# Three groups of seven block products in the feed-forward steps of a two-block transformer kernel on Trainium2

## The reference, cut to what matters

```
# D_MODEL = 2048, D_FF = 5632, SEQ = 256
h2 = rms_norm(x, g_norm2) * (1 + sc2) + sh2
x = x + gt2 * ((silu(h2 @ w_gate) * (h2 @ w_up)) @ w_down)            # first block
...
y = rms(h, norm_ffn_g_2)
h = h + (silu(y @ w_gate_2) * (y @ w_up_2)) @ w_down_2                # second block
```

## Time and profile before

| | |
|---|---|
| median of 3 runs | 2284.97 us (2284.89 to 2286.12) |
| profiled execution | span 2284.0 us, about 1 us around it up to the median |
| steps | 20, in two stretches from 536 to 1184 us and from 1524 to 2172 us |
| TensorE busy | 2234.5 us, 98% of the span |
| VectorE busy | 1894.3 us, 83% |
| ScalarE busy | 1164.2 us, 51% |
| DMA | 518.23 MB, mean 227 GB/s |
| granted TensorE clock | 0.9 or more in each of 40 slices |

### The profile page before, as it was taken

How to read it: one execution, slowest core, us unless ns; L and a number is a source line. 1 busy time by engine, 2 the same in 40 slices (tenths; PEclk the granted TensorE clock), 3 DMA queues, 4 the chain that set the end, 5 groups by cost and what they waited for, 6 DMA issues and landing times.

```text
span 2284.0 us, 30541 instructions
## 1 busy us (share of the span) xinstructions
PE 2234.5 (98%) x10404; PEld 1790.4 (78%) x10404; DVE 1894.3 (83%) x2265; ACT 1164.2 (51%) x1465; POOL 87.9 (4%) x124
## 2 busy tenths in 40 slices
PE   6999989999999999999999999999999999999998
PEld 3577657788888888888888887888888888888886
DVE  4376878989888888999995998589889999999866
ACT  3233367465445545555545444555555555555554
POOL 1100030000000000000010000000000000000020
PEclk9999999999999999999999999999999999999999
DMA  9999995856666656666656555666666566656564
GB/s 391 414 361 374 399 354 204 322 205 208 194 194 202 195 191 202 201 195 206 203 177 216 176 190 165 191 222 200 195 196 199 197 201 207 197 186 205 189 202 148
DMA packets 131565, 518.23 MB, mean 227 GB/s; under 512 B 14496, under 2 KB 20256, under 8 KB 118304
## 3 DMA queue, kind: packets, MB, share of 16 engines
q1 hardware_dynamic: 121552, 449.11, 58.8%
q0 software_dynamic: 9216, 67.11, 7.2%
q10 hardware_dynamic: 720, 0.99, 0.1%
HBM read 512.96 MB, written 4.19 MB: 226 GB/s over the span
## 4 chain that ended last, share of the span: by engine, by line
PE 77%; DVE 4%; issue 1%; ACT 1%; DMA 0%; DVEq 0%; SPq 0%; ACTq 0%
PE ps L2456 55%; PE ps L2638 20%; DVE w_lo L1930 1%; PE ps L2444 1%; PE ps L2602 1%; DVE gate L2199 1%; PE ps L2923 0%; DMA raw<-in_w_out 0%; ACT w_hi L888 0%; DVE fm_lo L1905 0%; DVE stage L1919 0%; PE ps L2332 0%; DVE ungated L1810 0%; DVE short L1382 0%; PE ps L2354 0%
## 5 line engine op out<-in xcount | busy, mean ns | idle before, releaser
L888 ACT ACTIVATE w_hi<-raw 128x1024 fp32r<-128x1024 f32 (+1 forms) x498 | 514.5, 1051 | 450.0 <-PE ps L2638 255.2
L1930 DVE TENSOR_TENSOR w_lo<-raw,w_hi 128x1024 fp32r<-128x1024 f32 (+1 forms) x248 | 299.5, 1218 | 152.4 <-ACT w_hi L888 147.5
L888 ACT ACTIVATE w_hi_more<-raw 128x1024 fp32r<-128x1024 f32 x264 | 278.9, 1056 | 209.0 <-DMA raw<-in_w_down 114.7
L2638 PE MATMUL ps<-w_lo,fm_hi 128*128 128x512 f32 (+1 forms) x896 | 347.2, 388 | 0.0
L2638 PE MATMUL ps<-w_hi,fm_hi 128*128 128x512 f32 (+1 forms) x840 | 332.1, 395 | 4.1 <-DVE w_lo L1930 2.7
L2456 PE MATMUL ps<-w_lo,fm_hi 128*128 128x512 f32 x800 | 311.3, 389 | 0.0
L2638 PE MATMUL ps<-w_hi,fm_lo 128*128 128x512 f32 (+1 forms) x776 | 300.3, 387 | 0.0
L1613 DVE TENSOR_TENSOR w_lo<-raw,w_hi_more 128x1024 fp32r<-128x1024 f32 x240 | 287.6, 1219 | 7.1
L1613 DVE TENSOR_TENSOR w_lo<-raw,w_hi 128x1024 fp32r<-128x1024 f32 x240 | 284.3, 1218 | 4.0
L2456 PE MATMUL ps<-w_lo,hid_hi 128*128 128x512 f32 x640 | 249.0, 389 | 0.0
L804 ACT ACTIVATE sum_w_hi<-sum_raw 128x1024 fp32r<-128x1024 f32 x120 | 126.9, 1058 | 174.5 <-DVE sum_raw L1640 121.9
(11 more groups left out here) (376 smaller groups left out, 3793.4 us busy)
## 6 DMA issues: line engine op xcount, KB each, us to landing
raw<-in_w_gate SPq DMA_DIRECT2D x176, 512.0 KB, 4.3
raw<-in_w_up SPq DMA_DIRECT2D x176, 512.0 KB, 3.5
raw<-in_w_down SPq DMA_DIRECT2D x176, 512.0 KB, 3.6
ada_raw<-in_w_ada POOLq DMA_DIRECT2D x64, 1024.0 KB, 10.6
raw<-in_w_in SPq DMA_DIRECT2D x120, 512.0 KB, 3.8
raw<-in_w_out SPq DMA_DIRECT2D x64, 512.0 KB, 3.6
ada_raw<-in_w_ada SPq DMA_DIRECT2D x16, 1024.0 KB, 8.4
ada_raw<-in_w_gate SPq DMA_DIRECT2D x16, 1024.0 KB, 5.8
```

The costliest lines, as they stand in the source:

```text
L888: act.activation(hi_tile(like)[:, :, 0:width], raw[:, slot, :, 0:width], ACT.Copy).then_inc(hi_ready, 1)
L1930: dve.tensor_tensor(w_lo[:, slot, :, 0:width], raw[:, slot, :, 0:width], hi_tile(p)[:, :, 0:width], ALU.subtract).then_inc(lo_dve, 1)
L2638: last = pe.matmul(banks[t][:, 0:width], a, b, start=kt == 0 and k == 0, stop=kt == kts - 1 and k == 2)
```

## The change

There are three groups, not two, so a step has 21 forms of 6 matmuls and four c pieces (270 matmuls, not 276). DVE makes four more sums and three more low parts of sums a step, ACT three more high parts. The third group's left-hand operands are made before the steps.

The work on the sums moves between engines. Before the down pieces of two banks ACT writes the running total into the banks (`sums_in`, SBUF to PSUM), PE accumulates onto it, and ACT copies the banks back (`sums_out`). DVE's `add_step` is gone. ACT applies Silu itself, DVE's `silu` is gone, and `hidden_next` is one multiplication.

The orders change too. In `early`, c1 no longer stands behind b22. In `middle`, one c piece stands in each of the first two groups, between w and z. The third group has none inside, and its w comes ahead of b21. Before the first step DVE now does `hidden_first` ahead of `early`, where it had stood inside it.

```
-GROUPS = 2
-STEP_ORDER = (("b11", 0), ("c", 0), ("v", 0), ("b22", 0), ("c", 1), ("u", 0), ("c", 2), ("b21", 0), ("w", 0), ("z", 0), ("c", 3),
-              ("b11", 1), ("v", 1), ("b22", 1), ("c", 4), ("u", 1), ("b21", 1), ("c", 5), ("w", 1), ("c", 6), ("z", 1), ("c", 7))
+GROUPS = 3
+STEP_ORDER = (("b11", 0), ("c", 0), ("v", 0), ("b22", 0), ("u", 0), ("b21", 0), ("w", 0), ("c", 1), ("z", 0),
+              ("b11", 1), ("v", 1), ("b22", 1), ("u", 1), ("b21", 1), ("w", 1), ("c", 2), ("z", 1),
+              ("b11", 2), ("v", 2), ("b22", 2), ("u", 2), ("w", 2), ("b21", 2), ("z", 2), ("c", 3))
...
+            def sums_in(i, d):
+                if d == 0:
+                    act.wait_ge(sum_copied, i * 2 + 2 * before + 2)
+                elif d == 1:
+                    act.wait_ge(drained, i + before + 1)
+                act.wait_ge(down_out, i * 4 + summed_to + (d - 3 if d < 2 else d - 1))
+                act.activation(down_banks(d), total[:, :, d * NW:(d + 1) * NW], ACT.Copy).then_inc(down_in, 1)
+            def sums_out(i, d):
+                act.wait_ge(pieces_used, i * 24 + a + 18 + 2 * d)
+                act.activation(total[:, :, d * NW:(d + 1) * NW], down_banks(d), ACT.Copy).then_inc(down_out, 1)
...
             def down_his(i):
+                down_hi(i, 0)
                 copy_first(i)
+                down_hi(i, 1)
                 copy_second(i)
+                sums_in(i, 0)
+                down_hi(i, 2, 3)
+                sums_in(i, 1)
+                down_hi(i, 4)
+                step_silu(i)
+                down_hi(i, 5)
+                sums_out(i, 0)
+                sums_in(i, 2)
+                down_hi(i, 6, 7)
+                sums_out(i, 1)
+                sums_in(i, 3)
...
-                    last = act.activation(silu_t[:, :, :], src, ACT.Tanh, scale=0.5)
+                    last = act.activation(hidden[:, :, :], src, ACT.Silu)
...
-                    last = dve.scalar_tensor_tensor(hidden[:, :, :], silu_t[:, :, :], 0.5, up, ALU.mult, ALU.mult)
+                    last = dve.tensor_tensor(hidden[:, :, :], hidden[:, :, :], up, ALU.mult)
...
-            def silu(i):
-                dve.wait_ge(tanh_done, i + done + 2)
-                dve.scalar_tensor_tensor(silu_t[:, :, :], silu_t[:, :, :], 1.0, sums[:, 0:2, :], ALU.add, ALU.mult).then_inc(silu_step, 1)
...
-            def add_step(i, d):
...
                 down_lows(i, (0,))
                 drain_forms(i)
                 up_sums(i)
-                down_lows(i, (1,))
-                down_lows(i, (2,))
+                down_lows(i, (1, 2))
                 gate_sums(i)
-                down_lows(i, (3,))
-                silu(i)
+                down_lows(i, (3, 4))
                 hidden_next(i)
+                down_lows(i, (5, 6, 7))
...
             mix_operands(1)
-            rests(f + UP + 2, f + UP + 4)
-            silu_first()
+            rests(f + UP + 2, f + UP + 3)
+            mix_operands(2)
+            rests(f + UP + 3, f + UP + 4)
...
-            first_lows(0)
+            hidden_first()
+            early(0)
```

More of the change, by code:

```diff
@@ L174, in hi_free, with last_in_place @@
     return p + 1 - (FFN_HI if f is not None and p - f >= FFN_HI else SPLIT)
-SUMMED = (("u", 0), ("v", 0), ("w", 0), ("z", 0), ("u", 1), ("v", 1), ("w", 1), ("z", 1))
+SUMMED = [(kind, k) for k in range(GROUPS) for kind in ("u", "v", "w", "z")]
 USED = [item for item in STEP_ORDER if item[0] in ("u", "w", "z")]
+def last_in_place(kind, k):
+    n, place = USED.index((kind, k)), sum_place(kind, k)
+    return next(m for m in range(n - 1, n - 1 - len(USED), -1) if sum_place(*USED[m]) == place)
 def low_by_dve(p):
@@ L426, in build @@
         unit_read, down_read = sem("unit_read"), sem("down_read")
+        down_in, down_out = sem("down_in"), sem("down_out")
         aux_filled, aux_drained = sem("aux_filled"), sem("aux_drained")
@@ L780, in act_ffn, with gate_silu, step_silu, down_banks @@
             a, before = f + 2 * UP, FFN_STEPS - 1 if done else 0
-            def gate_tanh(j, src):
+            total, summed_to = x if done else ungated, LEAD + 4 * before
+            def gate_silu(src):
                 if done:
                     for t in range(TT):
-                        last = act.activation(silu_t[:, t, :], src[:, t, :], ACT.Tanh, scale=x_half[:, t:t + 1])
+                        last = act.activation(hidden[:, t, :], src[:, t, :], ACT.Silu, scale=x_rstd[:, t:t + 1])
                 else:
-                    last = act.activation(silu_t[:, :, :], src, ACT.Tanh, scale=0.5)
-                last.then_inc(tanh_done, 1)
-            def step_tanh(i):
+                    last = act.activation(hidden[:, :, :], src, ACT.Silu)
+                last.then_inc(silu_done, 1)
+            def step_silu(i):
                 act.wait_ge(gate_read, i + done + 2)
-                gate_tanh(i + 1, sums[:, 0:2, :])
+                gate_silu(sums[:, 0:2, :])
+            def down_banks(d):
+                return ps[:, 4 + 2 * (d % 2):6 + 2 * (d % 2), :]
+            def sums_in(i, d):
[8 more added lines that the diff above has]
+                act.activation(total[:, :, d * NW:(d + 1) * NW], down_banks(d), ACT.Copy).then_inc(down_out, 1)
             def hidden_hi(n, dst=hid_hi, bank=0):
@@ L1628, in place_free @@
             def place_free(i, kind, k):
-                former = (kind, k - 1) if k and kind != "u" else (kind, k if kind == "u" else GROUPS - 1)
-                step_of = 1 if former[1] < k else 0
-                dve.wait_ge(form_used, (i + before + step_of) * 3 * GROUPS + USED.index(former) + 1)
+                dve.wait_ge(form_used, (i + before + 1) * 3 * GROUPS + last_in_place(kind, k) + 1)
             def sum_u(i, k):
@@ L1712, in middle @@
                 piece_low(i, "b21", 1)
-                piece_low(i, "c", 5)
                 sum_low(i, "w", 1)
-                piece_low(i, "c", 6)
+                piece_low(i, "c", 2)
                 sum_low(i, "z", 1)
-                piece_low(i, "c", 7)
+                sum_u(i, 2)
+                piece_low(i, "b11", 2)
+                sum_v(i, 2)
+                sum_w(i, 2)
+                piece_low(i, "v", 2)
+                piece_low(i, "b22", 2)
+                sum_low(i, "u", 2)
+                sum_z(i, 2)
+                sum_low(i, "w", 2)
+                piece_low(i, "b21", 2)
+                sum_low(i, "z", 2)
+                piece_low(i, "c", 3)
                 down_lows(i, (0,))
@@ L2451, in low_wait, with three_passes @@
                 pe.wait_ge(lo_dve if by_dve else lo_ready, i * LOWS_A_STEP[by_dve] + count)
-            def three_passes(bank, h, l, wh, wl, start, stop):
+            def three_passes(bank, h, l, wh, wl, start, stop, onto=False):
                 for k, (left, right) in enumerate(((h, wh), (l, wh), (h, wl))):
-                    last = pe.matmul(bank, left, right, start=start and k == 0, stop=stop and k == 2)
+                    last = pe.matmul(bank, left, right, start=start and k == 0, stop=stop and k == 2, skip_group_check=onto)
                 return last
@@ L2540, in down @@
                 for d in ds:
[L2541 to L2545 removed]
+                    pe.wait_ge(down_in, i * 4 + 4 * before + d + 1)
                     b = 4 + 2 * (d % 2)
```

162 lines of the change are left out of this document (63 added, 99 removed).

## The result

The changed kernel took 2382.94 us (median of 4 runs, 2381.54 to 2384.38), the kernel before 2285.36 beside it (median of 4, 2284.89 to 2286.12). The ratio is 1.0425, with a 95% interval of 1.0412 to 1.0438: slower by 4.3%. The forecast was 2371, with a range of 2345 to 2389. The profiled execution has a span of 2379.8 us, 95.8 more than before; it is the fastest of its four, and the medians lie 97.6 apart.

A forecast was written before the change was run, and what follows sets the result against it. It took DVE's written order and the turn to bound each step, not PE: 20 x 3.7 = 74 us, plus 12 at the block starts, is 86; 2285 + 86 = 2371 us, range 2345 to 2389.

The forecast's parts named there:

- The step: Each of 20 feed-forward steps: DVE's written order and the turn give 67.2 us, 3.7 more than now.
- the five places: PE waits for DVE at first b21 1.05, second v 1.3, second b21 0.6, third v 1.3, third w 0.65 us.
- DVE can't work ahead: In the down pieces DVE gets ahead only until the ring of six fills, then waits some 4 us for first v.
- the landing chain: Rival: the first v's landing, not the turn, holds DVE; 66.2 us a step, 2351 us; chance 0.09.
- the sum: Whole kernel: 20 x 3.7 = 74 for the steps and 12 for the block starts, 86 us more, 2371 us.
- a rival: The shorter chain, through the landing instead of the turn: 66.2 us a step, 2351 us; chance 0.09.
- 1.36 holds: DVE starts hid_lo 1.36 us after PE's first v, set by the turn, even with a landing of 4.8 us.
- PE as the bound: Rival: PE remains the bound in the steps, so fewer matmuls make the kernel faster, 2270 us; chance 0.12.
- ACT's queue: Rival: a PSUM copy or its wait holds a high part by 1 us; step 68.2, 2391 us; chance 0.06.
- The starts: Before each block's first step: 6.5 us more in the first block, 5.5 in the second, together 12.

The follow-up runs named there:

- the pair of extra instructions: Changed kernel plus one unused 1024-element DVE reduction a step: in the third group 2402.66 us, or between d5's and d6's low parts 2380.69 us.
- the halved low parts: Changed kernel with the low part of each sum made over 512 of 1024 elements, same number of matmuls: 2311.86 us, ratio 1.012.
- the shorter ring: Changed kernel with each transfer of the steps sent one piece later, as if the ring had five places: 2418.68 us, ratio 1.0582.
- the run with the earlier turn: Changed kernel with PE's turn of the hidden slice behind b11, not behind c0: 2367.79 us, ratio 1.0354 to the kernel before.
- the clean two groups: Changed kernel without its third group, in the orders of before, with the start and tail edits: 2286.47 us, ratio 1.0004 to the kernel before.
- the start woven: Changed kernel with `hidden_first` moved behind the low parts of b11 and c0 in each block's first step: 2372.53 us, ratio 1.0374.

## Why the prediction was right, and where it was off

**The step: right, in mechanism and size.** 67.2 was forecast and 67.24 measured; 74 us for the 20 steps against 74.5. Hid_lo starts 1.34 us behind the first v (forecast 1.36). D1 starts 43.18 behind the first v before it (863.76, and 887.82 less a step of 67.24), forecast 43.2. PE's waits by start times are 0.92, 1.15, 0.50, 1.16 and 0.52 at the five places, against 1.05, 1.3, 0.6, 1.3 and 0.65, and next to nothing at d1 (0.15). That is 4.25; the matmul behind each of these six restarts comes 0.1 later than usual, which makes 4.9 against the 5.05 of the forecast. That it is DVE's work at its place in the order that decides was shown by the pair of extra instructions (1.1 against 0) and by the halved low parts.

**DVE can't work ahead: right, with one term missing.** It waits 5.17 us for a landing, where some 4 was said, and the shorter ring made each step 2.1 us longer. The row from sum_u to hid_lo was put at 9.5 and took 10.0 in the run with the earlier turn. DVE's own instructions were sized well, 9.36; the missing term is the 0.45 for ACT's high part of the u sum. So the landing chain gives 66.7 a step, not 66.2, and in the changed kernel the turn holds DVE by 0.5 only. It didn't touch the sum, but two chains lie closer than I had them, and a rival was priced 10 us too low. The prediction also says that 1.36 holds with a landing of 4.8 too. It doesn't: 4.8 + 0.35 + 9.5 - 13.1 is 1.55.

**PE as the bound: failed, and why.** The Trainium skill (Perfetto Trace Analysis, Identifying the Most-Contended Engine) would have the engine with the highest occupancy optimized first. PE had 98%, its work fell by 1.36 us a step, and the kernel became slower. The prediction leaves out that the same section judges TensorE's headroom not by its matmuls' busy share but by its work against the peak and by the busy share of its weight loads. The share of the weight loads was 78% before, below DVE's 83%, and read so the section points at DVE. But the clean two groups took 118 us off DVE and were no faster. Neither share tells what this change does; both leave out the order in which the engines wait for each other. The sentence on consistent bubbles fits in part: PE loses the same 5 us in each step, and more when the ring is cut to five. That too few buffers make them is not shown, since they went down by 3.45 when DVE's low parts were halved, with the same ring.

**ACT's queue: hidden inside the steps, partly by luck, and wrong behind them.** Two groups with all of ACT's copies have steps as before. With three groups DVE waits 0.44 us a step for ACT's high part of the u sum, a place that the prediction does not name. It costs nothing only because the turn comes 0.47 later still. That is luck of 0.5 us, not a margin that was worked out. The copies of the running total into PSUM take 1.029 on average in the changed kernel, where 1.03 was taken. But I had looked at ACT's queue only inside a step. At the end of the last step a copy of the totals stands ahead of the high parts of the last slice, and the sum had nothing for that. 4.6 us were missing for the two tails; reordering gave 5.4 back.

**The starts: the place right, the size too small.** The forecast was 6.5 and 5.5, measured were 8.4 and 6.9. The waits are near the forecast: 0.82, 1.49 and 4.12 in the first block, 6.4 together, and 1.43 and 3.89 in the second. The missing term is the clock: behind 4 us of idle PE, b11 and c0 took 1.75 us longer. Its terms don't add up to their 6.5 either: 2.9 and 3.8, less 0.3, with 0.5 more, are 6.9. The 0.5 for a later hid_lo was not seen, the first step being 67.25 long like the others. The Trainium skill (TensorE: Matmul & The Clock Gate, What's actually happening) has half rate as the default state from which activity releases; the windows agree, with 0.50 granted behind the idle stretch. The forecast has no term for it. At the wait of 2.6 us behind the first block's last step the runs go both ways: 0.50 behind it in four profiled executions, 1.00 in four.

**The sum.** 74.5 + 15.3 + 4.6 + 1.4 is 95.8 against 86: half a us for the steps, 3 for the starts, 5 for the tails, and 1.4 that I can't tell from scatter. All of these have the same sign, so the measured time lies 12 us above the forecast of 2371, in the upper part of the range.

**What stays open.** A larger ring was not tried, so what the step would be without the landing chain is not measured. Nor was a part of DVE's low parts moved to GpSimd. Nor was another order of the same three groups: the prediction's own reading is that c pieces are where DVE catches up, and the third group has none inside. So it is not shown whether three groups must be slower, or only these three in this order. What sets their steps of 63.05 to 63.57 (PE's work with the turn is 63.46 before) was not taken apart.

## What to carry to other kernels

Where two engines hand work to each other in a written order, follow one period of it: start at an event that both share, count the instructions that stand in the queue up to each hand-over, and compare with when the other engine wants it. The sum of busy time tells only what the period can't go below; here one instruction more was free where the engine already waited for a buffer, and cost its full length in the stretch where the other engine waits for it. Then look at the two ends of the loop by themselves: what stands in an in-order queue ahead of the next part's first work, and what the granted clock is behind a wait there.

## What the runs showed of the hardware

A wait of PE of about 4 us (4.12 and 3.89 at the two starts) was followed by a granted clock of 0.50 for some us; waits of 0.3 to 1.0 us, five in each step, and single ones of 0.8 and 1.5 in the up pieces left it at 1.00. A wait of 2.6 us at the end of the first block had 0.50 behind it in four profiled executions and 1.00 in four. With the start woven, the clock at the same place stays at 1.00 and b11 and c0 take 4.51 us, as in the kernel before.

In the changed kernel copies of 1024 elements on ACT take 1.029 us from SBUF into PSUM and 1.018 from PSUM into SBUF, and Silu over 1024 elements takes 1.063, as Tanh had before. The second table costs one load:
```profile
515.15 1.28 ACT L797 ACT_TABLE_LOAD   x1
```
Silu is followed by copies and Silu again for 20 steps with no further load.

A matmul that restarts PE behind a wait has 0.34 us to its successor where 0.2268 is usual, so each short wait costs 0.1 us more than the start times of the two matmuls around it tell, and those tell 0.16 more than the idle column (1.157 - 0.227 = 0.93 at the first b21, where the column has 0.77).
